# Modulation matrix of a decoder layer in units of 128 whole rows, with six late units moved between projection tiles

## The reference, cut to what matters

```python
def modulation(c, w_ada, b_ada):              # c: 9 rows of 1024; w_ada: 1024 x 6144
    return jnp.split(jax.nn.silu(c) @ w_ada + b_ada, 6, axis=-1)

sh_m, sc_m, g_m, sh_f, sc_f, g_f = modulation(c_prompt, w_ada[l], b_ada[l])
h = rms_norm(x, norm_mix) * (1 + sc_m) + sh_m  # before the projection
z = h @ w_in                                   # q, k, v, u
# sliding-window attention of q, k, v; causal pooling mixer of u
x = x + g_m * (concat(attn, pool) @ w_out)
h = rms_norm(x, norm_ffn) * (1 + sc_f) + sh_f
y = x + g_f * moe(h)                           # top 4 of 32 experts
```

## Time and profile before

| | |
|---|---|
| median of 3 runs | 1338.39 us (1336.66 to 1340.96) |
| span of the profiled execution | 1334.0 us |
| median less span | 4.4 us |
| PE busy | 1206.5 us (90%) |
| DVE busy | 708.9 us (53%) |
| DMA | 474.16 MB, mean 355 GB/s |
| chain that ended last | PE 55%, DMA 14%, DVE 6% |

### The profile page before, as it was taken

The page is one execution under the profiler, slowest core; times in us unless marked ns, Lnnn a source line. Parts: engine busy times, 40 slices in busy tenths (PEclk is TensorE's granted clock), DMA queues, the critical chain, the costliest instruction groups (busy, mean ns, idle before and its releaser), DMA issues.

```text
span 1334.0 us, 17599 instructions
## 1 busy us (share of the span) xinstructions
PE 1206.5 (90%) x6394; PEld 717.5 (54%) x6394; DVE 708.9 (53%) x1111; ACT 489.3 (37%) x703; POOL 327.5 (25%) x353
## 2 busy tenths in 40 slices
PE   5899899969999979998899889998979998999974
PEld 2454455543675646754675257555447555565631
DVE  2533854563795765454784244536535536676631
ACT  5112422312565433333563133333423324455430
POOL 2214320130212314114213311143411134132211
PEclk8899999979999989999999999898989998999996
DMA  9953985299999999999999999999999999999994
GB/s 331 335 82 74 381 294 204 109 391 378 398 385 376 404 409 383 413 387 358 403 414 406 399 387 411 391 343 403 412 386 408 377 356 410 411 405 413 405 408 177
DMA packets 101740, 474.16 MB, mean 355 GB/s; under 512 B 17761, under 2 KB 20224, under 8 KB 55498
## 3 DMA queue, kind: packets, MB, share of 16 engines
q1 hardware_dynamic: 82282, 444.76, 83.2%
q0 software_dynamic: 18720, 26.54, 8.7%
q10 hardware_dynamic: 650, 1.72, 0.4%
HBM read 459.47 MB, written 32.66 MB: 369 GB/s over the span
## 4 chain that ended last, share of the span: by engine, by line
PE 55%; DMA 14%; DVE 6%; issue 2%; ACT 1%; SPq 1%; POOL 1%; POOLq 0%; DVEq 0%; ACTq 0%
PE bank L2420 52%; DMA raw<-in_w 7%; DVE rawr L2240 2%; DMA out_y_prompt<-gu,slot_tok 2%; DMA yd<-gu,idx_s 2%; PE bank L2468 1%; DMA yd<-ost,idx_s 1%; PE bank L2444 1%; ACT hi L2057 1%; POOL gu L1931 1%; DVE gu L2204 1%; DVE gu L2202 0%; DVE ost L2274 0%; SPq L547 0%; SPq L553 0%
## 5 line engine op out<-in xcount | busy, mean ns | idle before, releaser
L2240 DVE TENSOR_TENSOR rawr<-raw,hi 128x1024 fp32r<-128x1024 f32 x288 | 351.8, 1265 | 103.8 <-ACT hi L2057 102.2
L2057 ACT CAST hi<-raw 128x1024 fp32r<-128x1024 f32 x288 | 294.9, 1048 | 163.2 <-PE bank L2420 138.6
L1917 POOL DMA_INDIRECT yd<-ost,idx_s x31 | 56.5, 1822 | 324.8 <-ACT ost L2040 324.0
L2420 PE MATMUL bank<-raw,xT_even 128*64 128x512 f32 (+1 forms) x704 | 135.2, 600 | 0.1
L2420 PE MATMUL bank<-raw,aT 128*32 128x256 f32 (+1 forms) x992 | 113.5, 478 | 12.1 <-DMA raw<-in_w 12.1
L2420 PE MATMUL bank<-raw,xT_odd 128*32 128x512 f32 (+1 forms) x544 | 86.5, 659 | 15.2 <-DMA raw<-in_w 15.2
L2420 PE MATMUL bank<-hi,xTh_odd 128*128 128x512 f32 x224 | 76.9, 426 | 20.4 <-DVE rawr L2240 20.1
L2420 PE MATMUL bank<-hi,aTh 128*128 128x512 f32 x240 | 76.9, 402 | 12.7 <-DVE rawr L2240 12.7
L2420 PE MATMUL bank<-hi,xTh_even 128*128 128x512 f32 x256 | 83.4, 407 | 4.8 <-DVE rawr L2240 4.8
L2202 DVE TENSOR_SCALAR gu<-bank 128x512 f32<-128x512 f32 (+1 forms) x50 | 31.4, 628 | 103.2 <-PE bank L2420 103.2
L2022 ACT ACTIVATE gu<-gu 128x512 f32<-128x512 f32 (+1 forms) x50 | 29.2, 583 | 146.4 <-DVE gu L2202 146.4
(11 more groups left out here) (387 smaller groups left out, 1826.0 us busy)
## 6 DMA issues: line engine op xcount, KB each, us to landing
raw<-in_w SPq DMA_DIRECT2D x356, 1024.0 KB, 14.9
raw<-in_w SPq DMA_DIRECT2D x48, 512.0 KB, 13.2
raw<-in_w_ada SPq DMA_DIRECT2D x21, 1024.0 KB, 7.8
w_in_sb<-in_w_in SPq DMA_DIRECT2D x4, 1280.0 KB, 16.9
w_out_sb<-in_w_out SPq DMA_DIRECT2D x4, 1024.0 KB, 8.8
early<-in_w SPq DMA_DIRECT2D x4, 1024.0 KB, 12.4
ada_more<-in_w_ada SPq DMA_DIRECT2D x3, 1024.0 KB, 13.2
xs<-in_x_prompt SPq DMA_DIRECT2D x4, 512.0 KB, 13.9
```

Of the source, the lines that this page charges most:

```text
L1917: gp.indirect_dma_start(yd_of[n], bass.IndirectOffsetOnAxis(ap=m.idx_s[:, p % 6, b:b + 1], axis=0), out_rows(p, b), None, bounds_check=lim ...
L2057: nc.scalar.copy(m.hi[:, (2 * n + h) % HI, :], m.raw[:, slot, h * D:(h + 1) * D]).then_inc(hi_done, 1)
L2240: v.tensor_tensor(m.rawr[slot][:, half], m.raw[:, slot, half], m.hi[:, (2 * n + h) % HI, :].bitcast(F32), ALU.subtract).then_inc(lo_done, 1)
L2420: return nc.tensor.matmul(out, lhsT, rhs, start=start, stop=stop, skip_group_check=True)
```

## The change

A unit `n` is now 128 whole rows (`k = n % 8`) of one third of the columns (`j = n // 8`, 2048 columns), still 1 MB, 8 KB contiguous for a partition. The four column groups of the PE array take four chunks of 512 columns and accumulate over eight units in one bank, so that nothing is left to be added up but the bias, which is one DVE instruction over 128 partitions for a third. `cT` is padded to 32 columns with zeros. The first third is transposed by four full transposes after unit 7. There is one more place for units (slot 5 of `raw`). Units 8 to 11 are multiplied after the four projection tiles of the prompt, 12 and 13 after the first two pooling blocks, 14 and 15 in attention tile 0, three each in tiles 1 and 2, two in tile 3. `w_out` is loaded in one go behind unit 17, which waits only for unit 13's use. ACT issues four bias loads at its start, behind a DVE memset; POOL's wait before L688 is for another event. Left out of the listing are places of small tiles, the norm row `nf` in two parts, and counts of the same waits.

```diff
@@ -39,7 +39,8 @@
 RING = 13
-ADA_SLOTS, ADA_MORE = 3, 3
+ADA_RAW = (0, 1, 2, 5)
+ADA_SLOTS, ADA_MORE = len(ADA_RAW), 3
...
@@ -216,12 +218,11 @@
         m.vrow = at("vrow", [12, P], F32, s3 + 7680)
-        m.line = at("line", [NH, LINE], F32, raw0 + 4 * SLOT_B)
-        m.late_rows = at("late_rows", [9, 4 * D], F32, raw0 + 4 * SLOT_B)
-        m.crow = at("crow", [9, D], F32, raw0 + 4 * SLOT_B + 12288)
+        m.mod_rows = at("mod_rows", [P, 3, 512], F32, raw0 + 4 * SLOT_B)
+        m.line = at("line", [NH, LINE], F32, raw0 + 4 * SLOT_B + 6144)
+        m.crow = at("crow", [9, D], F32, raw0 + 6 * SLOT_B + 4096)
...
         m.ada_more = [at(f"ada_more{n}", [P, 2048], F32, H0 + place) for n, place in enumerate((81216, 89600, 41216))]
-        m.bada_01 = at("bada_01", [9, 2 * D], F32, H0 + 68928)
         m.xs = at("xs", [P, TT, D], F32, H0)
...
@@ -525,12 +524,10 @@
         a = ada_place(n)
-        return m.raw[:, a, :] if a < ADA_SLOTS else m.ada_more[a - ADA_SLOTS][:]
+        return m.raw[:, ADA_RAW[a], :] if a < ADA_SLOTS else m.ada_more[a - ADA_SLOTS][:]
...
         return 16 * (1 + sum(ada_place(k) == ada_place(n) for k in range(n)))
-
-    ada_bank = [bank[2 + c % 2] if c < 4 else bank[2 + 5 * (c % 2)] for c in range(CHUNKS)]
@@ -570,18 +567,19 @@
             def load_ada(n):
-                c, half = n // 2, n % 2
+                j, k = n // KC, n % KC
...
                     sp.wait_ge(s.ada_used, earlier[-1] + 1)
-                src = i["w_ada"][0, half * 512:(half + 1) * 512, c * 512:(c + 1) * 512]
-                sp.dma_start(ada_unit(n).rearrange("p (k n) -> p k n", k=4),
-                             src.rearrange("(k p) n -> p k n", p=P)).then_inc(ada_in[ada_place(n)], 16)
-
-            def store_mod(k):
-
-                sp.wait_ge(s.mr_ready, 2 * k + 6)
-                sp.dma_start(m.modd[k], m.late_rows[:, k * D:(k + 1) * D]).then_inc(s.mod_out, 16)
+                sp.dma_start(ada_unit(n), i["w_ada"][0, k * P:(k + 1) * P, j * 2048:(j + 1) * 2048]
+                             ).then_inc(ada_in[ada_place(n)], 16)
+
+            def store_mod(j):
+
+                sp.wait_ge(s.mr_ready, j + 1)
+                for q in range(4):
+                    sp.dma_start(m.modd[2 * j - 2 + q // 2, :, 512 * (q % 2):512 * (q % 2) + 512],
+                                 m.mod_rows[32 * q:32 * q + 9, j, :]).then_inc(s.mod_out, 16)
@@ -595,22 +593,18 @@
                 load_ada(n)
-                if n == WHOLE + 2:
-                    sp.wait_ge(s.skew_out, 16)
-                    sp.dma_start(m.late_rows[:], i["b_ada"][0:1, 2 * D:6 * D].to_broadcast([9, 4 * D])
-                                 ).then_inc(s.bada_in, 16)
-                if n in (12, 14, 16, 18):
-                    if n == 12:
-                        sp.wait_ge(s.z_ready, TT)
-                        sp.wait_ge(s.u_ready, 4)
-                    k = n - 12
-                    sp.dma_start(m.w_out[:, k:k + 2, :],
-                                 i["w_out"][0, k * P:(k + 2) * P, :].rearrange("(k p) n -> p k n", p=P)
-                                 ).then_inc(s.wout_in, 16)
-                if n >= 15 and n % 4 == 3:
-                    store_mod(n // 4 - 3)
+                if n == 17:
+                    sp.wait_ge(s.z_ready, TT)
+                    sp.wait_ge(s.u_ready, 4)
+                    for k in range(0, KC, 2):
+                        sp.dma_start(m.w_out[:, k:k + 2, :],
+                                     i["w_out"][0, k * P:(k + 2) * P, :].rearrange("(k p) n -> p k n", p=P)
+                                     ).then_inc(s.wout_in, 16)
+                if n == 20:
+                    store_mod(1)
+            store_mod(2)
             sp.wait_ge(s.bb_out, BB_ALL)
-            sp.wait_ge(s.mod_out, 3 * 16)
+            sp.wait_ge(s.mod_out, 8 * 16)
@@ -619,10 +613,8 @@
             load_bc(1, m.s2_bc)
-            store_mod(3)
-            for u in range(ADA_SLOTS):
+            for u in range(3):
                 load_unit(sp, 0, 0, u)
-            sp.wait_ge(s.mod_out, 4 * 16)
             load_unit(sp, 0, 0, 4)
@@ -684,7 +676,7 @@
                 gp.wait_ge(win_in[n], 16)
-            gp.wait_ge(s.mr_ready, WHOLE // 2)
+            gp.wait_ge(s.rel_ready, 1)
             gp.dma_start(m.bb[:, 0:2 * D], i["b1"][0]).then_inc(s.bb_in, 16)
...
@@ -831,7 +825,10 @@
                 act.dma_start(m.vrow[r:r + n, :], i[name][0].rearrange("(a b) -> a b", b=P)).then_inc(s.vecs_in, 16)
-            act.dma_start(m.bada_01[:], i["b_ada"][0:1, 0:2 * D].to_broadcast([9, 2 * D])).then_inc(s.bada_in, 16)
+            act.wait_ge(s.blank, 1)
+            for q in range(4):
+                src = i["b_ada"][0:1, :].rearrange("o (j q n) -> o q j n", j=3, q=4)[:, q]
+                act.dma_start(m.mod_rows[32 * q:32 * q + 9, :, :], src.to_broadcast([9, 3, 512])).then_inc(s.bada_in, 16)
             act.wait_ge(s.c_in, 32)
...
@@ -1046,28 +1042,25 @@
+            v.memset(m.mod_rows[:], 0.0).then_inc(s.blank, 1)
             v.memset(m.eps[:], EPS).then_inc(s.eps_ready, 1)
+            v.memset(m.cT[:], 0.0).then_inc(s.blank, 1)
...
             v.wait_ge(s.c_tr, 1)
-            v.tensor_copy(m.cT[:].rearrange("p k n -> p (k n)"), bank[6][:, 0:72]).then_inc(s.cT_ready, 1)
-            def mod_row(c):
-
-                v.wait_ge(s.ada_used, 2 * c + 2)
-                v.wait_ge(s.bada_in, 16 if c < 4 else 32)
-                if c in (2, 3):
-                    v.wait_ge(s.mt_tr, c - 1)
-                shift = m.bada_01[:, c * 512:c * 512 + 512] if c < 4 else m.late_rows[:, (c - 4) * 512:(c - 3) * 512]
-                row = m.mrow[:, c % 2, :] if c < 4 else shift
-                added = v.tensor_tensor(row, ada_bank[c][0:9, :], shift, ALU.add)
-                for q in range(1, 4):
+            v.wait_ge(s.blank, 2)
+            v.tensor_copy(m.cT[:, :, 0:9], bank[6][:, 0:72].rearrange("p (k n) -> p k n", n=9)).then_inc(s.cT_ready, 1)
+
+            def mod_row(j):
+
+                v.wait_ge(s.ada_used, KC * (j + 1))
+                v.wait_ge(s.bada_in, 4 * 16)
+                row = m.mod_rows[:, j, :]
+                added = v.tensor_tensor(row, bank[2][:], row, ALU.add)
+                if j == 2:
                     step(added)
-                    added = v.tensor_tensor(row, row, ada_bank[c][32 * q:32 * q + 9, :], ALU.add)
-                if c in (8, 9):
-                    step(added)
-                    v.wait_ge(s.nf_in, 16)
-                    added = v.scalar_tensor_tensor(row, row, 1.0, m.nf[:, c % 2 * 512:c % 2 * 512 + 512], ALU.add,
-                                                   ALU.mult)
+                    v.wait_ge(s.nf_in, 2 * 16)
+                    added = v.scalar_tensor_tensor(row[0:64], row[0:64], 1.0, m.nf[:], ALU.add, ALU.mult)
@@ -1079,8 +1072,6 @@
                                   bank[1][:].rearrange("p (k n) -> p k n", k=4)).then_inc(s.xT_dve, 1)
-                if t in (2, TP):
-                    mod_row(t // 2 - 1)
             v.wait_ge(s.x_tr, 2 * TT)
@@ -1088,11 +1079,11 @@
             v.tensor_copy(m.relrep[:], m.relb[:]).then_inc(s.rel_ready, 1)
-            mod_row(2)
-            mod_row(3)
-
-            v.wait_ge(s.mt_tr, 4)
-            v.tensor_copy(m.modT[:].rearrange("p c n -> p (c n)"), bank[7][:, 0:144]).then_inc(s.modT_ready, 1)
+            mod_row(0)
+
+            v.wait_ge(s.mt_tr, 1)
+            v.tensor_copy(m.modT[:].rearrange("p (q b) n -> p q b n", b=4),
+                          bank[7][:].rearrange("p (b q n) -> p q b n", b=4, q=4)[:, :, :, 0:9]).then_inc(s.modT_ready, 1)
             v.wait_ge(s.modT_ready, 1)
@@ -1218,11 +1209,11 @@
                     maxima(t + 1)
-                mod_row(2 * t + 4)
+                if t in (0, TP - 1):
+                    mod_row(1 if not t else 2)
                 normed(t)
...
                     sums(t + 1)
-                mod_row(2 * t + 5)
@@ -1359,15 +1350,13 @@
-                c, half = n // 2, n % 2
+                j, k = n // KC, n % KC
                 pe.wait_ge(ada_in[ada_place(n)], ada_landed(n))
-                if not half and c >= 2:
-                    pe.wait_ge(s.mr_ready, c - 1)
-                if not half and c >= 4 and c % 2:
-                    pe.wait_ge(s.sc_used, 4 * min((c - 1) // 2, TP))
-                for k in range(4):
-                    last = mm(ada_bank[c][32 * k:32 * k + 9, :], m.cT[:, 4 * half + k, :],
-                              ada_unit(n)[:, k * 512:(k + 1) * 512], start=half == 0, stop=half == 1)
+                if j and not k:
+                    pe.wait_ge(s.mr_ready, j)
+                for q in range(4):
+                    last = mm(bank[2][32 * q:32 * q + 32, :], m.cT[:, k, :], ada_unit(n)[:, q * 512:(q + 1) * 512],
+                              start=(k == 0), stop=(k == KC - 1))
                 last.then_inc(s.ada_used, 1)
@@ -1383,27 +1372,16 @@
-            def turn_mod(c):
-
-                pe.wait_ge(s.mr_ready, c + 1)
```

(47 more changed lines are left out.)

11 lines of the change are left out of this document (2 added, 9 removed).

## The result

The changed kernel takes 1345.68 us (median of 9 runs, 1340.80 to 1349.10) against 1338.39 (9 runs, 1333.02 to 1340.96). The ratio is 1.0053, 95% interval 1.0035 to 1.0070: 7.1 us slower by the ratio, where 1337.0 was forecast and 1343.5 was the range's upper end. The profiled execution has a span of 1344.3 us.

The account below looks back on a forecast made before the run. The head was taken as bound by DVE's additions at the start, then PE's own work and the softmax chain, not transfers. Terms -2.9 + 4.9 + 0 - 4.4 + 1.0 = -1.4 us gave 1337.0 us, range 1331.5 to 1343.5.

Parts of the forecast that it names:

- part 2: At `turn_qk(0)`: the chain from `bb` ends at 64.35, PE comes at 63.8; 2.9 us early, bounds -1.8 to -3.5.
- part 1: Start, up to the copy of `modT`: fewer DVE additions and 8 KB rows gain 4.5 us, between 3.4 and 5.6.
- part 6: Clock: a longer PE gap before 144.69 may start attention tile 1 at 1.2 GHz; +1.0 us, between 0 and 2.0.
- part 3: Six units in the projection cost 0.98 us each; one already counted, five more make +4.9 us.
- Nothing: Start: the `mod_rows` memset and four bias issues on ACT delay the silu some 2 us, costing PE nothing.
- The 1.1 us for rows of 8 KB: Start: units in 8 KB rows transfer 8.4 MB in 20.3 us against 21.5, landing up to 1.1 us earlier.
- Part 4: Projection: moved units delay the `skew` store 6.7 us, inside the slack of its chain; 0, up to +4.8 us.
- the skew rival: Slower: the `skew` store ends over 8.6 us later and PE loses 4.8, plus one for `bd`; 1342.8 us, chance 0.13.
- the slack of 8.6: Samples' `qk_ready` before PE wants it at `turn_qk(TP)`: 5.5, plus 2.0 for later PE, plus 1.1 for the earlier store.
- Part 5: Attention stage: fewer units per tile and no transfer waits save 4.4 us, bounds 2.4 and 6.4.
- The rival: Clock, slower: PE at 1.2 GHz at `turn_qk(0)`, tile 1 and tile 3; +7.0 us, 1344.0 us, chance 0.10.

Follow-up runs that it names:

- the kernel with 12 rows: The changed kernel with the bias loaded once as 12 rows of 2 KB and added by TensorE, DVE only copying the bank: 1341.69 us, ratio 1.0027.

## Why the prediction was wrong

At `mix_out` the forecast was 1.4 us early; it is 9.0 us late. The 10.4 us between them split at two points of the table (forecast -2.9 and +2.0 there): 3.5 up to `turn_qk(0)`, 2.4 up to `turn_qk(TP)`, 4.5 in the attention stage. By cause, two steps failed: the late `bb` chain made 3.5 of it (part 2; a term of part 1 that was put at nothing is behind most of that), and the half clock made some 6.3, 1.7 behind `turn_qk(0)` and 4.6 in tile 1 (part 6). The price of a unit made 0.7 (part 3).

**Part 1, right in the chain; the failed term is "Nothing".** The copy of `modT` ended at 37.95 (37.8 forecast ahead of the gain from the rows): the lean addition is worth what was said. The 1.1 us for rows of 8 KB are not there: unit 7 landed at 34.99, as before, and `w_in` 1.2 us later. The part put the four bias issues at nothing, and they took it: in the kernel without them unit 7 landed 2.3 us and `w_in` 1.4 us earlier than before the change, and the kernel with 12 rows issued `bb` 1.1 us earlier. The Trainium skill's page "DMA: Bandwidth & Descriptors", section Specifications, asks for at least 512 B in a transfer to reach the line rate, which the rows have before and after. On the sum of the changed kernel that came out right, but the trace does not agree with it: rows of 8 KB ran at 422 GB/s in 16 to 20 us, those of 2 KB at 394.

**Part 2, a failed step: the chain came later, not earlier.** It was put at 64.35; `kd` was there at 67.75. That is 3.4 us: `bb` was issued 1.2 us later instead of 1.1 earlier, and ACT's cast followed the second load's issue after 8.1 us, where it was 7.0 before. The bounds assumed that `w_in` lands no later than before. I had counted the bias loads as issue time on ACT and not as transfers; the runs without them and with 12 rows show them as the cause of 2.3 to 2.6 us. The 8.1 us behind the issue they don't explain: it is 8.0 and 8.3 us in those two runs. Its 1.1 us stay open.

**Part 3, a little too small.** From `turn_qk(1)` to `turn_qk(2)` lie 12.17 instead of 10.97 us, so a unit between projection tiles costs 1.2, not 0.98: 0.99 to the next matmul's start, 0.1 more ahead of the unit and 0.1 in the first pair of matmuls behind it. What makes these two tenths isn't shown. Five make 5.65 instead of 4.9.

**Part 4, right in the result, with luck in it.** The `skew` store ended at 101.47, 6.6 us later (5.6 forecast: 6.7 less 1.1), and `kd` of the samples at 126.36 against PE's 130.56, so PE didn't wait and the skew rival is out here. But that chain ended 9.2 us later than before, more than the slack of 8.6: had PE come at the forecast 124.7, it would have waited 1.7. The moved units make 6.8 of the 9.2, since with the units in their old places `kd` ended at 119.58; 3.7 of that lie in the `skew` store, 3.1 behind it. Where PE was made early the samples' chain did end last: `turn_qk(TP)` at 127.42 after a wait of 0.9 us, and at 127.15 after 2.3.

**Part 5, right.** From `turn_qk(TP)` to `mix_out` the stage took 66.5 instead of 65.4 us. Without the 5.6 us that tile 1 took longer it is 4.4 us shorter, as forecast; tiles 2 and 3 alone are 4.6 us shorter (4.0 forecast).

**Part 6, mis-sized.** The gap was foreseen, at 4.5 us (it is 5.9), but its price was taken from a single row, which holds 4 us. The cold stretch lasted 12 us and cost 5.6; I took 1.0, at most 2.0. With the gap filled the same tile took 14.1. Another 1.7 came behind the wait at `turn_qk(0)`, which the forecast had at full clock. The rival named the two places that were hit first and said 1344.0; it was right in the main thing, at a chance of 0.10. That its time is so near is partly luck: it priced tile 1 at 2.0 too and left out the 3.5 us of the chain, and it took 4.0 us for a tile 3 that wasn't cold, where PE's only wait is 0.84 us.

What stays open: the profiled executions also differ by 2.7 us between the first expert weights and the end, and no experiment touched that. In those of the experiments it is 1044.3 to 1049.5 us, with 1045.2 before and 1047.9 after, so it may be no more than the spread of runs.

## What to carry to other kernels

A gap that an edit opens on TensorE costs more than its length: price the work behind it at half clock until a row shows the clock back, and look where work without a due time could fill it. A small load on a second queue is to be counted by what it takes from the main stream at the moment it runs, and not by its bytes or by its issue time; here that was 1.5 to 4.5 times its bytes. And before a gain at the start is carried on, ask of each later wait what chain holds it, and recompute that chain's own start.

## What the runs showed of the hardware

- With gaps of 4.0 to 5.9 us on TensorE before tile 1 the granted clock was 0.50, the lower level, in 4 to 12 us of nearly unbroken matmuls behind them; in two of these traces it was down ahead of the gap. With gaps of 0 to 2.1 us at the same place tile 1 ran at 1.00 in the profiled executions. Where the clock was down ahead of the fill, it came back within the fill: 0.50 in 148 to 152 us, 0.68 in 152 to 156, 1.00 from 156, with 22 multiplications from 151.34 to 157.92.
- 216 KB of broadcast rows went with about 1 MB less of transfer over 8 us (286 and 298 instead of some 415 GB/s), with the DMA share at 0.99 and 1.02 all the while. 384 KB of `bb` did the like, 0.6 MB less at 40 to 44 us (271 and 275 GB/s), in rows of 4 and 8 KB that are not broadcast. 24 KB in 12 rows did nothing that can be seen (402 GB/s). Whether it is the second queue, the rows or the source isn't shown.
- DVE and POOL seem to hold each other up in some pairs: `dTs` 128x32 on DVE took 0.19 us beside a `TENSOR_SCALAR` of POOL (the kernel before and the changed one), but 1.85 us where POOL issued a transfer and then ran a `TENSOR_TENSOR`, and both ended within 0.1 us of each other. That is read from times that coincide; no run tested it.
